# A hybrid decoder trunk: part of the counting of a top-k search given to ScalarE

## The reference, cut to what matters

```python
def indexer_scores(iq, iw, ik):
    s = jax.nn.relu(jnp.einsum('bthd,bsd->bths', iq, ik).astype(jnp.float32))
    return jnp.einsum('bths,bth->bts', s, iw.astype(jnp.float32)) * (IDX_DIM ** -0.5 * IDX_HEADS ** -0.5)
...
        sc = indexer_scores(iqb, iwb, ik)
        adm = key_pos[None, :] <= qpos[:, None]
        sc = jnp.where(adm[None], sc, -jnp.inf)
        _, idx = lax.top_k(sc, topk)
        valid = idx <= qpos[None, :, None]
        return attend_selected(qb, k[bi, idx], v[bi, idx], valid)
```

## Time and profile before

| what | value |
|---|---|
| time, median of 3 runs | 2327.97 us (2327.13 to 2329.59) |
| profiled execution, span from first to last instruction | 2320.0 us |
| TensorE, VectorE, ScalarE, GpSimd busy | 2024.6, 1044.0, 689.4, 584.9 us |
| chain that ended last | TensorE 48%, issue 20%, VectorE 18%, GpSimd 6%, ScalarE 4% |
| prompt search counts (L1247), 186 | 175.9 us of VectorE |
| the same line, sample, 31 | 41.4 us of VectorE |

### The profile page before, as it was taken

One profiled execution on the slowest core, in us unless ns is written; L12 is line 12 of the kernel. 1 busy time (PEld: TensorE's weight loads), 2 busy tenths in 40 slices (PEclk: granted clock), 3 DMA queues, 4 the chain that ended last, 5 costly groups with the idle time before them and its releaser, 6 DMA issues.

```text
span 2320.0 us, 33486 instructions
## 1 busy us (share of the span) xinstructions
PE 2024.6 (87%) x12384; PEld 1790.7 (77%) x12384; DVE 1044.0 (45%) x1948; ACT 689.4 (30%) x924; POOL 584.9 (25%) x311
## 2 busy tenths in 40 slices
PE   4999999999999998996797779998767788779698
PEld 3998999999999997995643579898333445579598
DVE  4114333211244403316488666788798821231522
ACT  4233333122433312323463112222433422221310
POOL 3333333554333454442100011111000000025221
PEclk8999999999999998997887889999888987789899
DMA  4222222222223232013102221122100005321221
GB/s 132 82 73 74 80 73 73 74 80 81 82 81 90 81 90 93 27 36 115 46 1 46 61 62 32 31 76 92 53 1 0 0 24 150 123 105 45 65 66 39
DMA packets 240507, 152.74 MB, mean 66 GB/s; under 512 B 24946, under 2 KB 235634, under 8 KB 240050
## 3 DMA queue, kind: packets, MB, share of 16 engines
q1 hardware_dynamic: 229314, 140.74, 20.5%
q10 hardware_dynamic: 10192, 9.46, 1.3%
q0 software_dynamic: 928, 1.62, 0.3%
HBM read 135.33 MB, written 16.43 MB: 65 GB/s over the span
## 4 chain that ended last, share of the span: by engine, by line
PE 48%; issue 20%; DVE 18%; POOL 6%; ACT 4%; SPq 2%; DMA 1%; DVEq 0%; POOLq 0%; ACTq 0%
PE PS L373 36%; POOL wlo L363 4%; PE PS L1828 3%; DVE acc L1247 3%; PE PS L1596 2%; DVE sc L1235 2%; POOL acc L605 1%; PE PS L1854 1%; PE PS L1543 1%; DVE hlo L417 1%; ACT swp L833 1%; PE PS L1879 1%; DVE rbc L405 1%; SPq L551 1%; POOL vs L604 1%
## 5 line engine op out<-in xcount | busy, mean ns | idle before, releaser
L363 POOL TENSOR_TENSOR wlo<-wraw,whi 128x1024 fp32r<-128x1024 f32 x177 | 430.8, 2434 | 949.3 <-ACT whi L358 942.5
L373 PE MATMUL PS<-hhi_g,whi 128*128 128x288 f32 (+1 forms) x1536 | 326.7, 294 | 14.6 <-POOL wlo L363 7.6
L373 PE MATMUL PS<-hhi_g,wlo 128*128 128x288 f32 (+1 forms) x1536 | 320.3, 290 | 0.0
L373 PE MATMUL PS<-hlo_g,whi 128*128 128x288 f32 (+1 forms) x1536 | 319.3, 289 | 0.0
L373 PE MATMUL PS<-hhi,whi 128*128 128x364 f32 x1176 | 273.8, 343 | 40.5 <-DVE hlo L417 19.0
L358 ACT ACTIVATE whi<-wraw 128x1024 fp32r<-128x1024 f32 x177 | 186.5, 1055 | 340.8 <-PE PS L373 313.7
L373 PE MATMUL PS<-hlo,whi 128*128 128x364 f32 x1176 | 267.8, 337 | 0.0
L373 PE MATMUL PS<-hhi,wlo 128*128 128x364 f32 x1176 | 267.4, 337 | 0.0
L373 PEld LDWEIGHTS PS<-hhi_g,whi 128*128 128x128 f32 x1536 | 242.4, 190 | 17.9 <-issue 12.1
L373 PEld LDWEIGHTS PS<-hhi,whi 128*128 128x128 f32 x1176 | 212.0, 197 | 48.6 <-issue 25.0
L373 PEld LDWEIGHTS PS<-hlo_g,whi 128*128 128x128 f32 x1536 | 243.4, 190 | 0.0
(11 more groups left out here) (308 smaller groups left out, 2706.3 us busy)
## 6 DMA issues: line engine op xcount, KB each, us to landing
wraw<-in_w_in_a_dram SPq DMA_DIRECT2D x96, 512.0 KB, 3.8
wraw<-in_w_out_a_dram SPq DMA_DIRECT2D x32, 512.0 KB, 3.8
wraw<-in_w_in_b_dram SPq DMA_DIRECT2D x25, 512.0 KB, 3.6
wraw<-in_w_pe_gate_dram SPq DMA_DIRECT2D x16, 512.0 KB, 4.0
kpg<-in_cache_k_dram SPq DMA_DIRECT2D x64, 128.0 KB, 2.0
vpg<-in_cache_v_dram SPq DMA_DIRECT2D x64, 128.0 KB, 2.0
xs<-xT SPq DMA_DIRECT2D x1, 4368.0 KB, 13.0
xT<-xs SPq DMA_DIRECT2D x1, 4368.0 KB, 13.3
```

What stands on the lines that cost most here:

```text
L363: nc.gpsimd.tensor_tensor(wlo[par][:], wraw[par][:], whi[par][:].bitcast(F32), ALU.subtract).then_inc(w_lo, 1)
L373: mm = nc.tensor.matmul(o, w[par][:, k, :], r(k, c0, cn), start=first and k == 0 and n == 0, stop=last and k == KD - 1 and n == 2)
```

## The change

ScalarE gets a function `Sign(thr - x)` with an accumulator, which gives the number of scores below the threshold less the number above it. For each prompt bit it counts blocks 6 and 7 (896 and 1024 columns), VectorE counts blocks 2 to 5, now the scores below the threshold; for each sample bit ScalarE counts all 1088 columns. `keep_bit` compares with a limit per column of `kth`, which GpSimd writes once, in two operations instead of one. A score equal to the threshold counts neither way in a signed count, so the search of those rows can end one value low; `above` tries the next value once more with an exact count on VectorE, for the two prompt blocks after the 31 bits and for the sample in step 56.

The signed counts are written into ScalarE's queue by `prompt_counts(t)` and `sample_counts(t)`: after the Relu of each sample (bits 0 to 7), after the roots of each key head, after the copy of each value tile, after the swap of each query unit, ahead of the split of each of the z units (two bits each, one in the sixth), and, for the sample, in each of steps 25 to 55 behind Exp(n) and the copies of n - 1. Each waits for VectorE's threshold, and VectorE's `keep_bit` waits for the count.

```diff
@@ -229,7 +229,10 @@
         repb = pl("repb", [NS, DEC_B, NS], BF16)
         tbit, cand, mbit = (pl(n, [P, 7], U32) for n in ("tbit", "cand", "mbit"))
         bitc = pl("bitc", [P, 7], U32)
-        sgn, thr, cnt, need = (pl(n, [P, 7]) for n in ("sgn", "thr", "cnt", "need"))
+        sgn, thr, cnt, need, kth, ge = (pl(n, [P, 7]) for n in ("sgn", "thr", "cnt", "need", "kth", "ge"))
+        step = pl("step", [P, 3], I32)
+        vdmp = acc[:].bitcast(BF16)[:, 0:TP]
+        admp = acc[:].bitcast(BF16)[:, TP:2 * TP]
         pl = region(H1, H1 + NH * TP * 4)
         iqT = pl("iqT", [P, IH // 2, TP])
         csI, snI = pl("csI", [P, TP]), pl("snI", [P, TP])
@@ -328,6 +331,18 @@
         ikp = [sem(f"ikp{q}") for q in range(3)]
         ss_ = {n: sem(f"ss_{n}") for n in ("pre", "tr", "ev", "mm", "re", "sum", "wt", "cp", "ok")}
         cs_ok = sem("cs_ok")
+        bit_thr, bit_cnt, lim_ok = sem("bit_thr"), sem("bit_cnt"), sem("lim_ok")
+        sbit_thr, sbit_cnt = sem("sbit_thr"), sem("sbit_cnt")
+
+        VBLK, ABLK = range(2, 6), range(6, NBLK)
+
+        def area(b):
+            return sc[:, block_off(b):block_off(b + 1)]
+
+        def limit(j):
+
+            n = SLS if j == NBLK - 2 else (j + 3) * P
+            return n - TOPK + 0.5 if j + 2 in VBLK else n - 2 * TOPK + 0.5
         z_ev, z_in = sem("z_ev"), [sem(f"z_in{f}") for f in range(KD)]
         z_st = [sem("z_st0"), sem("z_st1")]
         at_ = {n: sem(f"at_{n}") for n in ("s", "mx", "nb", "ex", "nr", "tr", "pt", "pv", "o")}
@@ -658,6 +673,9 @@
                 split_lo(pool, (U_IQ + f + 1) % 2, U_IQ + f + 1)
             split_lo(pool, 1, U_K)
             own.link(nc.gpsimd.memset(caus[:], 0.0))
+            for j in range(NBLK - 1):
+                own.link(nc.gpsimd.memset(kth[:, j:j + 1], limit(j)))
+            pool.sem_inc(lim_ok, 1)
             nc.gpsimd.affine_select(out=caus[:, P:2 * P], in_=caus[:, P:2 * P], compare_op=ALU.is_ge, fill=-BIG,
                                     base=0, pattern=[[-1, P]], channel_multiplier=1).then_inc(cs_ok, 1)
             pool.wait_ge(xs_out, 16)
@@ -870,6 +888,21 @@
                 nc.scalar.activation(pring[m % 2][:, 0:n], PS[:, m % 6, 0:n], ACT.Relu).then_inc(sc_re, 1)
 
 
+            def prompt_counts(t):
+
+                act.wait_ge(bit_thr, t + 1)
+                for j, b in enumerate(ABLK):
+                    if j:
+                        act.wait_ge(bit_cnt, 2 * t + j)
+                    nc.scalar.activation(admp[:, 0:(b + 1) * P], area(b), ACT.Sign, bias=thr[:, b - 2:b - 1],
+                                         scale=-1.0, accum_out=cnt[:, b - 2:b - 1]).then_inc(bit_cnt, 1)
+
+            def sample_counts(t):
+
+                act.wait_ge(sbit_thr, t + 1)
+                nc.scalar.activation(admp[0:NS, 0:SLS], scs[:], ACT.Sign, bias=thr[0:NS, 6:7], scale=-1.0,
+                                     accum_out=cnt[0:NS, 6:7]).then_inc(sbit_cnt, 1)
+
             def ikT_evac(b):
                 act.wait_ge(ss_["tr"], b + 1)
                 if b >= 2:
@@ -886,6 +919,7 @@
                 if b:
                     act.wait_ge(ss_["sum"], b)
                 nc.scalar.activation(rels[:], PSF[0:NS, 3 * BANK:3 * BANK + SLS], ACT.Relu).then_inc(ss_["re"], 1)
+                prompt_counts(b)
 
 
             for g in range(NKV):
@@ -899,6 +933,7 @@
                 nc.scalar.activation(as3(sqt[:]), slot3(u % 2), ACT.Square).then_inc(kk_["swa"], 1)
                 swap(swp, u % 2, DH // 2, gqk[:, 1:2]).then_inc(kk_["swa"], 1)
                 roots(1 + g, DH)
+                prompt_counts(EARLY_BITS + g)
 
             for g in range(NKV):
                 u = U_V + g
@@ -908,6 +943,7 @@
                 if g:
                     act.wait_ge(tt_tr, 12)
                 nc.scalar.activation(as3(sqt[:]), slot3(u % 2), ACT.Copy).then_inc(kk_["vev"], 1)
+                prompt_counts(EARLY_BITS + NKV + g)
 
             act.wait_ge(tt_tr, 15)
             with act.Fori(0, NH // 2) as i:
@@ -921,9 +957,13 @@
                     slot = (U_Q + ff) % 2
                     nc.scalar.activation(as3(sqt[:]), slot3(slot), ACT.Square)
                     swap(swp, slot, DH // 2, gqk[:, 0:1]).then_inc(qq["swa"], 1)
-
+                    prompt_counts(EARLY_BITS + KV_BITS + f)
+
+            LATE = EARLY_BITS + KV_BITS + NH
             act.wait_ge(qq["add"], 9)
             for f in range(KD):
+                for t in range(LATE + 2 * f, min(LATE + 2 * f + 2, BITS)):
+                    prompt_counts(t)
                 split_hi(act, (U_Z + f + 1) % 2, (U_Z + f + 1) // 2 + 1, U_Z + f + 1)
                 act.wait_ge(w_used, U_Z + f + 1)
                 if f >= 2:
@@ -956,6 +996,8 @@
                                      scale=qs[:, 1 + b, h:h + 1], accum_out=asm[:, n:n + 1]).then_inc(at_["ex"], 1)
                 if n:
                     pieces_out(n - 1)
+                if SIDE <= n < SIDE + BITS:
+                    sample_counts(n - SIDE)
             pieces_out(len(STEPS) - 1)
 
 
@@ -1260,24 +1302,54 @@
                 own.link(nc.vector.tensor_scalar(sgn[r, c], sgn[r, c], 2.0, -1.0, ALU.mult, ALU.add))
                 own.link(nc.vector.memset(bitc[r, c], 1 << 30))
 
-            def search_bit(group):
-                r, c = slice(0, group[0]), group[1]
+            def try_bit(r, c):
+
                 own.link(nc.vector.tensor_tensor(cand[r, c], tbit[r, c], bitc[r, c], ALU.bitwise_xor))
-                own.link(nc.vector.tensor_tensor(thr[r, c], cand[r, c].bitcast(F32), sgn[r, c], ALU.mult))
-                count(group, ALU.is_ge, thr)
-
-                own.link(nc.vector.scalar_tensor_tensor(mbit[r, c], cnt[r, c], TOPK - 0.5, bitc[r, c], ALU.is_ge, ALU.mult))
+                return nc.vector.tensor_tensor(thr[r, c], cand[r, c].bitcast(F32), sgn[r, c], ALU.mult)
+
+            def keep_bit(r, c):
+
+                own.link(nc.vector.tensor_tensor(ge[r, c], cnt[r, c], kth[r, c], ALU.is_le))
+                own.link(nc.vector.tensor_tensor(mbit[r, c], ge[r, c], bitc[r, c], ALU.mult))
                 own.link(nc.vector.tensor_tensor(tbit[r, c], tbit[r, c], mbit[r, c], ALU.bitwise_xor))
                 own.link(nc.vector.tensor_scalar(bitc[r, c], bitc[r, c], 1, None, ALU.logical_shift_right))
 
-            BIT_LINKS = 5 + len(PROMPT[2])
-
-            def search_bits(trips):
+            PCOLS, SCOLS = (slice(0, P), slice(0, NBLK - 2)), (slice(0, NS), slice(NBLK - 2, NBLK - 1))
+
+            def search_bit(t):
+                try_bit(*PCOLS).then_inc(bit_thr, 1)
+                dve.wait_ge(bit_thr, t + 1)
+                for b in VBLK:
+                    own.link(nc.vector.tensor_scalar(vdmp[:, 0:(b + 1) * P], area(b), thr[:, b - 2:b - 1], None,
+                                                     ALU.is_lt, ALU.add, accum_out=cnt[:, b - 2:b - 1]))
+                dve.wait_ge(bit_cnt, 2 * t + 2)
+                keep_bit(*PCOLS)
+
+            BIT_LINKS = 5 + len(VBLK)
+
+            def search_bits(first, trips):
                 with dve.Fori(0, trips) as i:
                     own.enter(i, BIT_LINKS)
-                    search_bit(PROMPT)
+                    search_bit(first + i)
                 own.leave(trips)
 
+            def above(group):
+
+                r, c = slice(0, group[0]), group[1]
+                a = slice(c.start + (len(VBLK) if group is PROMPT else 0), c.stop)
+                w = slice(0, a.stop - a.start)
+                z = step[r, w]
+                own.link(nc.vector.tensor_scalar(z, tbit[r, a].bitcast(F32), 1.17549435e-38, -1.0, ALU.is_ge, ALU.mult))
+                own.link(nc.vector.tensor_tensor(tbit[r, a].bitcast(I32), tbit[r, a].bitcast(I32), z, ALU.bitwise_and))
+                own.link(nc.vector.tensor_copy(z, sgn[r, a]))
+                own.link(nc.vector.tensor_tensor(cand[r, a].bitcast(I32), tbit[r, a].bitcast(I32), z, ALU.add))
+                own.link(nc.vector.tensor_tensor(thr[r, a], cand[r, a].bitcast(F32), sgn[r, a], ALU.mult))
+                for j in range(a.start, a.stop):
+                    x = group[2][j - c.start]
+                    own.link(nc.vector.tensor_scalar(vdmp[r, 0:x.shape[1]], x, thr[r, j:j + 1], None,
+                                                     ALU.is_ge, ALU.add, accum_out=cnt[r, j:j + 1]))
+                own.link(nc.vector.scalar_tensor_tensor(z, cnt[r, a], TOPK - 0.5, sgn[r, a], ALU.is_ge, ALU.mult))
+                own.link(nc.vector.tensor_tensor(tbit[r, a].bitcast(I32), tbit[r, a].bitcast(I32), z, ALU.add))
 
             RESOLVE_AT = [(0, 1), (2, 3), (4,), (5,), (6,), (7,), (), ()]
 
@@ -1305,8 +1377,9 @@
                     own.link(nc.vector.tensor_scalar(out, cum, 1.0, BIG, ALU.subtract, ALU.mult))
 
             dve.wait_ge(sc_ok, NBLK - 2)
+            dve.wait_ge(lim_ok, 1)
             start_search(PROMPT)
-            search_bits(EARLY_BITS)
+            search_bits(0, EARLY_BITS)
             dve.wait_ge(ss_["sum"], DEC_B)
```

(18 more changed lines are left out.)

## The result

The changed kernel takes 2348.31 us (median of 4 runs, 2347.21 to 2349.57), the kernel before 2327.55 us in the same runs (2327.04 to 2329.59): ratio **1.0096**, 95% interval 1.0082 to 1.0109. It is slower by 20.8 us; 2356 was forecast.

The account below looks back on a forecast made before the run. TensorE was taken to set the z projection, VectorE the q projection and attention steps. Span 2320.0 - 4 (earlier stages) + 32 (attention steps 25 to 56) = 2348, with 8.0 from span to median 2356 us; range 2334 to 2373.

Parts of the forecast that it names:

- 24 plain steps: Attention steps 25 to 56: +0.26 us for each of 16 plain steps, 4.0, less 0.7 for step 25.
- eight long steps: Steps ending a group of four heads: value product late behind count and exponential; four at +4.2, four at +3.0: 28.8 us.
- from span to median: Whole kernel: the shown runs' median stands 8.0 us above the profiled span, added to 2348 to give 2356 us.
- Earlier stages: Stages up to the first mask: query units gain, z units give it back; sum -4 us, bounds -14 and +4.
- The hold by GpSimd's split: Query units: VectorE's small two-input operations after the counts wait for GpSimd; cycle 14.9 us, without the hold 12.6.
- the ring: Attention steps: count waits for VectorE's threshold, scaling for ScalarE's exponential; closed loop of 4.6 us against 4.3 before.
- the bound of +24: Lower bound for attention steps 25 to 56: count 1.25 us and a ring costing the plain steps nothing.
- (a): Attention steps: ScalarE's count fits its idle time, the ring does not close, VectorE's relief passes through; 2305 us, chance 0.12.
- (b): The ring as said, but earlier stages give more and the value product takes 6 us, not 8; 2338 us, chance 0.10.
- (c): Whole kernel: the halves cancel if copies are not delayed; 2328 us, chance 0.04.
- (e): Whole kernel: lower clock and late z units; 2372 us, chance 0.09.
- (d): Sign needs a table load, 62 x 1.28 us on the ring and some in prompt bits; 2436 or more, chance 0.03.

Follow-up runs that it names:

- the prompt's part alone: Changed kernel with the sample's bits back on VectorE, only the prompt's two widest counts on ScalarE: 2321.5 us, ratio 0.9987 to the kernel before.
- the sample's part alone: Changed kernel with all six prompt counts back on VectorE, only the sample's counts on ScalarE: 2356.48 us, ratio 1.0130 to the kernel before.
- the z run: The late count, with ScalarE splitting the next z unit's weights ahead of its two prompt counts: 2284.33 us, ratio 0.9826 to the kernel before.
- the doubled and the short count: Changed kernel with each sample count made twice, ratio 1.0232; or with an extra 256-column count ahead of each, ratio 1.0150, to the kernel before.
- the copies first: Changed kernel, but in steps ending a group of four heads ScalarE copies the transposed pieces ahead of the count: ratio 0.9985 to the kernel before.
- the late count: Changed kernel with each sample count issued one step later, behind the next step's exponential and copies: 2295.08 us, ratio 0.9868 to the kernel before.
- the threshold early: Changed kernel with VectorE's keep_bit and try_bit moved ahead of the step's reciprocal and scaling: ratio 0.9929 to the kernel before.
- the late count with the short extra: The late count plus an extra 256-column count ahead of each sample count on ScalarE: ratio 0.9902 to the kernel before.

## Why the prediction was right

The sign, the place and the mechanism held; the forecast was 8 us too high, of which 6.5 is the last row of the table. The agreement of the rest is better than its parts, since the plain steps were put 2.7 us too high and the long ones 1.8 too low.

| step of the prediction | forecast | profile after |
|---|---|---|
| copy of the sample's scores | 1292.1 | 1291.97 |
| first q unit | 1377.7 | 1377.74 |
| eighth rotation | 1495.3 | 1495.20 |
| second z unit, behind it | +24.2 | +24.0 |
| first mask | 1613 | 1613.45 |
| 24 plain steps | +3.3 | +0.6 |
| eight long steps | +28.8 | +30.6 |
| value product in step 51 | 7.5 into it | 7.1 |
| from span to median | +8.0 | +1.5 |

**Earlier stages: right, for reasons partly right.** The hold by GpSimd's split behind the counts, a rotation every 14.7 us on the mean (forecast 15.1), and the z units' late start are in the rows above. The start of the search itself was 1.5 us later in this execution (1234.61 against the earlier trace rows), ahead of anything that changed, so the stages gained 4.9 and not 3.4. A further 3.1 us is at step 20: one value product of 6 matmuls took 5.49 us in the profile before, at a granted clock of 0.50 (1.2 GHz), and 2.84 after, at 1.00 (2.4 GHz); no edit touches it. The run with the prompt's part alone puts the whole gain at 3.1 us by medians, the changed kernel against the sample's part alone at 7.9 by the ratios. Had I read the split's place as a choice and not as given, the 9.4 us would have stood out as a loss to be undone; the z run shows that they were on the path.

**Plain steps: the ring was there, its price too high.** (The forecast of +3.3 was for 16 of these 24.) I put 1.35 us for the count and 1.27 for the exponential, 4.6 for the ring. In the rows of steps 51 and 52 the exponential follows the count's start by 1.20 (the read of the sum runs beside it) and the reciprocal follows the exponential's start by 1.24: with the 1.9 of scaling and small operations 4.34 us, which is also what step 54, without resolving, takes (1847.28 to 1851.62). I had 4.3 for before, where this step took 4.43 (1828.53 to 1832.96). So the ring cost the plain steps 0.03 us each and not 0.26, and 1.20 lies outside my bounds of 1.25 and 1.44, since I counted 0.14 us for the read of the sum, which in fact adds nothing to the distance from the count's start to the exponential's. That the ring is closed all the same is shown by the doubled and the short count (1.19 and 0.49 us in each plain step) and by its opening, which takes 30.1 us from those steps.

**Long steps: right.** +30.6 against 28.8; the run with the copies first takes back 30.2 of it with nothing else in the code moved. The trace tells its two parts apart. The eight products start 3.4 us later in their steps on the mean, 27.4 in sum (2.6 us into the step before, 6.0 after): 3.7 in the four with resolving and 3.1 in the others, where I had put 4.2 and 3.0. They also take longer, 57.2 us in sum and not 51.6: the one of step 51 8.93 us and not 8.02, the next 9.08 and not 6.28. These 5.6 us, at a granted clock of 0.77 and not 0.85, stood in my sum only as a bound. Some 2 us less elsewhere in these steps make up the rest.

**From span to median: the term that was off.** I carried 8.0 us from the profiled execution before over to the changed kernel, and called it what lies around the instructions. In every timed execution of the changed kernel the time stands 1.7 to 1.8 us above that execution's own span (2348.5 against 2346.8), and so it does in the executions timed for the experiments. By that measure the profiled execution before, with a span of 2320.0, took some 2321.7 us, less than any timed one of that kernel (the lowest is 2322.47). So of the 8.0 us some 6.3 were the luck of one execution.

**Slips in my sums.** 4.6 less 4.3 is 0.3 for the ring, not 0.26; the bound of +24 adds up to +25.7; and the copy of the sample's scores comes out at 1292.0, not 1292.1. None changes the forecast by more than 1 us.

**The rivals.** (a), the relief passing through, was refused for this order of the queue, and it is what the late count makes of it: 2295, even below the 2305 worked out. (b), (c) and (e) differ from the forecast in sizes only, and the measured time lies between (b), 2338, and the forecast: the product did not get shorter, as (b) needs. (d), a table load per Sign, is out: no load stands at L897 or L903, and the pair of counts is at 2.4 us with none between. The page "ScalarE: Activation LUTs" of the Trainium skill (Table sets) doesn't list sign among the fillers; the trace shows it at no cost beside Exp, and beside Silu and Sqrt, whose own loads are as many as before.

## What to carry to other kernels

When work goes to an engine that looks empty, ask where in its in-order queue the new instruction stands, what it waits for, and who waits behind it; here the same instruction one place further back made a loss of 21 us a gain of 30. If the two engines wait for each other once in each step, the sum of both is the step, and the relief of one is gone: price the ring, and double the suspect to see whether each step pays. Look at the steps one by one, since an extra that only the shortest steps pay speaks of a full engine and not of a ring. A long product on TensorE hides extra work in its own step, but whatever feeds it, here two copies of half a microsecond, must stand ahead of work that is only side work.

## What was not expected of the hardware

- The Sign with its accumulator held the next instruction on ScalarE back by 1.20 us for 64x1088: that is the Sign's own duration, and the 0.19 us of reading the sum (1828.32 to 1828.51) lie across the next start (1828.41) and add nothing. Over 1024 columns from SBUF a plain copy takes 1.05 us, the Sign 1.15 and the exponential 1.24, as the prediction took it from the number of pointer operands; whether these are the reason, no run isolates.
- TensorE's granted clock differed much between orders of the same work. In the same stretch, with the same 387 matmuls, it was 0.77 with 132.2 us busy in the changed kernel, 0.85 with 125.0 before, 0.91 with 116.6 with the threshold early, and 0.94 with 112.8 with the late count. TensorE idled least in the last (32 us) and most in the first (71), but the order is not strict: the late count with the short extra idled 39 us at 0.89, the early threshold 43 at 0.91. What of the time the clock itself is worth, no run isolates.
- GpSimd's split of 2.38 us holds VectorE's two-input operations on 6 columns too: 2.30 us where 0.17 is usual. The Trainium skill (SBUF — State Buffer, Who interferes with whom) has the rule; the trace agrees, for an operation of 6 columns as for one of 1092 (3.25 us where 1.30 is usual).
